# Making the low half of each weight slot in two VectorE instructions instead of one

## What is computed

```
proj = rms_norm(x) @ w_in          # block 1: 2048 x 12288, then RWKV-7 mixing and band attention
x = x + rms_norm(merged @ w_out)
proj = rms_norm(x) @ w_in_2        # block 2: sparse attention, spatial gating
x = x + merged @ w_out_2;  x = x + relu(h @ w_ff1)**2 @ w_ff2
...                                # block 3: pooling, attention, another MLP
```

## Time and profile before

| | before |
|---|---|
| median of 3 runs (lowest, highest) | 3455.51 us (3454.36, 3463.07) |
| span of the profiled execution | 3455.6 us |
| TensorE busy | 3366.9 us, 97% |
| VectorE busy | 2204.8 us, 64%, of which L2436 1368.9 us |
| ScalarE busy | 1543.8 us, 45% |
| GpSimd busy | 295.2 us, 9% |
| granted TensorE clock, mean | 0.992 |

### The profile page before, as it was taken

How to read it: one execution, slowest core, us unless ns; L and a number is a source line. 1 busy time by engine, 2 the same in 40 slices (tenths; PEclk the granted TensorE clock), 3 DMA queues, 4 the chain that set the end, 5 groups by cost and what they waited for, 6 DMA issues and landing times.

```text
span 3455.6 us, 52015 instructions
## 1 busy us (share of the span) xinstructions
PE 3366.9 (97%) x21718; PEld 2908.9 (84%) x21718; DVE 2204.8 (64%) x3040; ACT 1543.8 (45%) x2121; POOL 295.2 (9%) x318
## 2 busy tenths in 40 slices
PE   8999999999989999999999999999999999999998
PEld 7888877778878888888888888888888888888887
DVE  5567655556667576777666446655777866446654
ACT  4454433334543455544544334444454544334443
POOL 3100122220011111100100000001000100000000
PEclk9999999999989999999999999999999999999999
DMA  6554433335535545655555656555544556556554
GB/s 193 180 178 151 138 111 116 107 107 195 190 123 171 187 154 169 193 164 173 182 193 186 193 185 192 187 191 188 166 159 159 183 184 207 194 183 195 192 198 146
DMA packets 550751, 592.98 MB, mean 172 GB/s; under 512 B 16757, under 2 KB 511733, under 8 KB 550262
## 3 DMA queue, kind: packets, MB, share of 16 engines
q1 hardware_dynamic: 550518, 589.66, 52.7%
HBM read 583.24 MB, written 6.32 MB: 171 GB/s over the span
## 4 chain that ended last, share of the span: by engine, by line
PE 87%; DVE 7%; ACT 2%; issue 2%; DMA 1%; POOL 0%; SPq 0%; DVEq 0%; ACTq 0%; POOLq 0%
PE gp L2526 45%; PE gp L2530 24%; PE gp L2511 7%; PE sidep L1115 4%; PE gp L2516 3%; DVE w_parts L2436 2%; ACT w_parts L2429 1%; DVE stage L2143 0%; DMA high<-bias_rows 0%; PE sidep L570 0%; ACT lo_half L2037 0%; PE sidep L1355 0%; DVE stage L2139 0%; DMA ring<-w_branch_rwkv 0%; DVE low L2175 0%
## 5 line engine op out<-in xcount | busy, mean ns | idle before, releaser
L2436 DVE TENSOR_TENSOR w_parts<-ring,w_parts 128x1024 fp32r<-128x1024 f32 x1084 | 1368.9, 1285 | 452.8 <-ACT w_parts L2429 451.5
L2526 PE MATMUL gp<-x_parts,w_parts 128*128 128x512 f32 x5840 | 1481.7, 398 | 11.1 <-issue 5.5
L2429 ACT ACTIVATE w_parts<-ring 128x1024 fp32r<-128x1024 f32 x1084 | 1109.8, 1053 | 453.5 <-PE gp L2516 188.9
L2526 PEld LDWEIGHTS gp<-x_parts,w_parts 128*128 128x128 f32 x5840 | 1061.7, 190 | 215.6 <-issue 13.4
L2530 PEld LDWEIGHTS gp<-x_parts,w_parts 128*128 128x128 f32 x5840 | 771.8, 191 | 48.0 <-issue 6.7
L2530 PE MATMUL gp<-x_parts,w_parts 128*128 128x256 f32 x5840 | 801.4, 285 | 2.8 <-DVE w_parts L2436 2.6
L2037 ACT ACTIVATE lo_half<-gp 128x512 f32<-128x512 f32 x239 | 142.8, 598 | 892.1 <-PE gp L2526 459.4
L2526 PE MATMUL gp<-ff_parts,w_parts 128*128 128x512 f32 x1792 | 430.8, 391 | 0.0
L2526 PEld LDWEIGHTS gp<-ff_parts,w_parts 128*128 128x128 f32 x1792 | 328.6, 188 | 63.0
L2139 DVE TENSOR_TENSOR stage<-gp,lo_half 128x512 f32<-128x512 f32 x168 | 116.2, 692 | 377.3 <-ACT lo_half L2037 376.4
L2511 PE MATMUL gp<-w_parts,ff_parts 128*128 128x512 f32 x1024 | 273.7, 389 | 0.0
(11 more groups left out here) (392 smaller groups left out, 1867.1 us busy)
## 6 DMA issues: line engine op xcount, KB each, us to landing
ring<-w_in SPq DMA_DIRECT2D x220, 1024.0 KB, 5.1
ring<-w_ff SPq DMA_DIRECT2D x128, 1024.0 KB, 5.6
ring<-w_up SPq DMA_DIRECT2D x64, 1024.0 KB, 6.0
ring<-w_down SPq DMA_DIRECT2D x64, 1024.0 KB, 5.0
ring<-w_out SPq DMA_DIRECT2D x48, 1024.0 KB, 5.3
ring<-w_branch_attn SPq DMA_DIRECT2D x8, 1024.0 KB, 5.2
ring<-w_branch_rwkv SPq DMA_DIRECT2D x8, 1024.0 KB, 5.2
gate_scratch<-stage SPq DMA_DIRECT2D x16, 256.0 KB, 2.2
```

Of the source, the lines that this page charges most:

```text
L2429: act.activation(w_parts[:, q % PARTS, 0], ring[:, u % RING, SLOT * (q % 2):SLOT * (q % 2) + SLOT, :], ACT.Copy).then_inc(high_split, 1)
L2436: v.tensor_tensor(w_parts[:, q % PARTS, 1], ring[:, u % RING, SLOT * (q % 2):SLOT * (q % 2) + SLOT, :], w_parts[:, q % PARTS, 0].bitcast(F ...
L2526: return pe.matmul(gp[:, k % 2, j, :, :], w_parts[:, q % PARTS, 0, c, j * P:(j + 1) * P], operand(s, b, SLOT * n + c), start=(n == 0 and c ...
```

## The change

`split_low` gets a third argument, `part_of_slot`. It makes only half of the slot's low part, two chunks of 128x256 (so 128x512 numbers in one instruction). Part 0 waits for the high part; part 1 signals `low_split`. VectorE's main loop calls it twice for each slot, and between the calls it runs the mixer steps that are due at q + 0.17. Nothing changes for the other engines but the semaphores' timing.

```diff
-        def split_low(v, q):
+        def split_low(v, q, part_of_slot):
             if q >= n_slots:
                 return
-            u = q // 2
-            v.wait_ge(high_split, q + 1)
-            v.tensor_tensor(w_parts[:, q % PARTS, 1], ring[:, u % RING, SLOT * (q % 2):SLOT * (q % 2) + SLOT, :],
-                            w_parts[:, q % PARTS, 0].bitcast(F32), ALU.subtract).then_inc(low_split, 1)
+            u, c, w = q // 2, SLOT // 2 * part_of_slot, SLOT // 2
+            if part_of_slot == 0:
+                v.wait_ge(high_split, q + 1)
+            m = v.tensor_tensor(w_parts[:, q % PARTS, 1, c:c + w],
+                                ring[:, u % RING, SLOT * (q % 2) + c:SLOT * (q % 2) + c + w, :],
+                                w_parts[:, q % PARTS, 0, c:c + w].bitcast(F32), ALU.subtract)
+            if part_of_slot:
+                m.then_inc(low_split, 1)
...
                     side.run(q)
-                    split_low(v, q + 2)
+                    split_low(v, q + 2, 0)
+                    side.run(q + 0.17)
+                    split_low(v, q + 2, 1)
                     if ended(q) and not last_of_section(q):
                         sums_vector(v, *ended(q), 1)
                     side.run(q + 0.34)
```

More of the change, by code:

```diff
@@ L457, in start_vector @@
                 if g == 3:
-                    split_low(v, 0)
+                    for part_of_slot in range(2):
+                        split_low(v, 0, part_of_slot)
             for g in range(4, 8):
@@ L2576, in _ @@
                 side.run(-1)
-                split_low(v, 1)
+                for part_of_slot in range(2):
+                    split_low(v, 1, part_of_slot)
                 for q in range(n_slots + 1):
```

## The result

The changed kernel took 3475.96 us in the median of 4 runs (3472.40 to 3479.43), the kernel before 3457.82 us in 4 (3454.36 to 3463.07). The ratio is 1.0049, with an interval of 1.0035 to 1.0063: slower by 0.5%, where 3459 within 3450 to 3470 was forecast. The time is near that of the second rival (3472.9), and the largest single part of it is that rival's mechanism, but in six places of which none was on its list.

The account below looks back on a forecast made before the run. TensorE was taken as the bound, busy for 3366.9 of 3455.6 us. Adding 3.4 for spacing and 2.8 for GpSimd between halves, less 2.7 for moved steps, gave 3459.1, forecast as 3459 us, range 3450 to 3470.

Parts of the forecast that it names:

- the second rival: In 13 places the second half waits for a whole GpSimd instruction, 16.6 us: 3472.9 us; chance 0.19.
- 47: Low halves in VectorE's unbroken work behind TensorE's existing waits; each 0.073 us later, 3.4 us together.
- 15 slots only: Slots of 1084 whose low half ends below 0.5 us before its first low product; the median is 3 to 12.
- the 13 of the 47: Exposed low halves with GpSimd's work beside them, where a GpSimd turn between the halves could cost 0 to 16.6 us.
- 0.7 us in four places: Cost of GpSimd getting in between the halves, by L940's own 0.66 us: 2.8 us, range 0 to 16.6.
- Slots there stand ready over 8 us ahead, so that is hidden.: Behind the roots, the second half, L2143 and ScalarE's next steps come some 2.5 us later, at no cost.
- The roots' gain: At 807 us the roots (L1055) start 1.25 us earlier; TensorE's wait shrinks from 2.37 to 1.12 us.
- The spacing: Two halves take VectorE 0.073 us more per slot than one low half, 79 us in all, 3.4 on TensorE.
- The clock: 0: Shifts of half-clock stretches on TensorE counted as 0 us, with -1.7 and +3.4 for the range.
- GpSimd gets in between: A waiting GpSimd instruction runs whole between the halves in 13 places, 16.6 us: 3472.9 us; chance 0.19.
- The places pay: All four TensorE waits with a moved step vanish, 5.3 us, and the half-clock stretch at 807: 3452.0 us; chance 0.12.
- VectorE the bound: VectorE's extra 79 us come onto the path where it is full: 3534.6 us; chance 0.03.

Follow-up runs that it names:

- e10: Kernel before, with two halves and nothing between them in only six slots, the fourth of blocks 2 to 7 of down2_1: 3467.48 us, ratio 1.0025.
- e4: Kernel before, with halves directly behind one another only in the 64 slots of down2_1: 3466.10 us, ratio 1.0014.
- e7: Changed kernel, with GpSimd's adds behind blocks 1 to 6 of out2, down2_1 and out3a held until the next needed low half is made: 3467.34 us, ratio 1.0025.
- e1: Changed kernel, with halves but no place for mixer steps between them in any slot: 3482.31 us, ratio 1.0064.
- e3: Changed kernel, with halves only in the 34 slots that have steps between them, one instruction in the other 1050: 3456.98 us, ratio 1.0000.
- e5: Changed kernel, with GpSimd's adds of squares behind down2_1 replaced by a one-column write (norm not the reference's): 3469.86 us, ratio 1.0031.
- e6: Changed kernel, with GpSimd's two adds behind each block of down2_1 replaced by four memsets that read nothing: 3470.17 us, ratio 1.0036.
- e8: Changed kernel, with each slot in four instructions of 128x256 and nothing between them: 3505.00 us, ratio 1.0135.
- e2: Kernel before, whole low halves kept, with the mixer steps due at q + 0.17 run ahead of them: 3459.80 us, ratio 1.0001.
- e9: Kernel before, with two halves and nothing between them in 464 slots of nine sections where idle time had grown little or not: 3457.51 us, ratio 0.9999.

## Why the prediction was wrong

**Which low halves are exposed: the step that failed.** I counted the low halves behind waits that were already there, down to 0.06 us, and got 47. The six slots of down2_1 had no wait before that the profile shows; their low half ended 0.15 us before its products began. The 0.15 is also what lies between the end and the products where TensorE does wait for a low half (before, 826.62 to 826.76; after, 2355.83 to 2355.98), so there was no slack at all. They were among the "15 slots only" below 0.5 us, which I read as a sign of safety and did not price. The mechanism had been found, with the right moment ("a waiting GpSimd instruction gets in as soon as one VectorE instruction ends"), and it was weighed only on the 13 of the 47 with GpSimd beside them. For these six slots the price was in the trace: a GpSimd add of 1.30 us (2339.95) with nothing to hide it. Measured, it is 1.22 us, six times, 7.3 us. With that the sum would have been 3466, just past what can be told from no change. e10, e4 and e7 show it from three sides.

**The price of a place elsewhere.** I took 0.7 us in four places. The idle time at two grew by about 0.6 us, 461 and 657. At 657 us in after:
```profile
658.50 1.11 DVE L2438 TENSOR_TENSOR w_parts<-ring,w_parts 128x512 fp32r<-128x512 f32 x1 [0.80 <-ACT w_parts L2430]
659.02 1.17 POOL L952 TENSOR_TENSOR high<-high 128x256 f32<-128x256 f32 x1
659.53 1.21 DVE L2438 TENSOR_TENSOR w_parts<-ring,w_parts 128x512 fp32r<-128x512 f32 x1
661.49 0.27 PE L1116 MATMUL sidep<-high 64*64 64x64 f32 x2 [1.90 <-DVE high L1027]
```
The second half starts at 659.53 and takes 1.21 us, 0.5 of them behind L952. e1 has the same two (0.62 and 0.58), so price and mechanism were right, and the number of places was two, not four. The argument that a half is blocked no longer than a whole held for the first half alone: the second is blocked once more. At the wait behind L997, from which the 0.7 was read and where it was to show, the idle time grew by 0.06. The 0.82 us of L997 is also of another kind than the 2.19: L997 has one SBUF input, and the sentence on two inputs beside which the prediction sets it doesn't cover it.

**"Slots there stand ready over 8 us ahead, so that is hidden."** Wrong. The roots' gain of 1.27 us came as forecast (1.10 us left, 1.12 forecast), but the 2.5 us by which the rest moved back took 1.1 to 1.35 us of it again at 826. I had looked at the stock at the roots and not followed it to where it runs out. Likewise 0.46 came back at 570.9 and 0.35 at 1099. Of 2.8 us gained, about 0.6 stayed; e3, which has these and little else, ended 0.7 us of idle time below before, and the time doesn't show it.

**The spacing.** 0.073 us a slot was right. On TensorE I counted 3.4 us; the small places sum to 4.7, some of them without a wait before. Not all of these are spacing: 0.6 of them, at 1016 us, is 0 in e5 to e7, where all slots are halved too. The wait for GpSimd at 1029 us grew from 0.29 to 1.97 in after and e1, but to 0.45 in e5, e6 and e7; it follows the clock ahead of it, as shown above.

**"The clock: 0."** The stretch at half clock behind the roots went, and others came. Two stretches of after by window (length, busy by engine with counts, granted clock, DMA share, GB/s), as the earlier trace rows:
```profile
812.90:816.30 3.40, 3.00 (x25) 2.49 (x26) 2.41 (x6) 1.82 (x3) 0.00 (x0) 1.00 0.00 0
793.50:796.90 3.40, 3.40 (x43) 3.02 (x43) 2.16 (x6) 0.00 (x0) 0.00 (x0) 0.58 0.00 0
```
Over all executions the mean granted clock was 0.9906 for before (27 runs; 0.9905 and 0.9911 beside the later kernels), 0.9895 for after, 0.9876 for e1, 0.9893, 0.9886 and 0.9895 for e5 to e7, and 0.987 for e8. It was 0.9901 to 0.9911 for e2, e3, e4, e9 and e10. So it falls only in the kernels in which the slots of all sections are cut. 0.0011 of 3455 us is 3.8 us for after, from four runs that lie between 0.988 and 0.991, so its size is rough; 0.0030 is 10.4 for e1. That fits e1's 22.4 us over before against after's 18.1, with less idle time, though the intervals of the two ratios overlap. e7 adds up: 4.5 us of idle time and 3.5 of clock are 8.0, measured 8.4. That the small waits in the remaining sections do it is argued from this pattern and not shown, and which of them would, no run here tells apart.

**The rivals.** "GpSimd gets in between" is what happened, in other places and at half the size: 8.5 us (7.3 and 1.2) against its 16.6 for 13 places. That its 3472.9 is near the measured time is luck; what came back behind the moved steps, the small waits and the clock make up the remainder. "The places pay" fails by what is given back (e2: 5.1 us shrunk, 0.6 kept). "VectorE the bound" fails by its size: VectorE works for 84.9 us more and the span grew by 16.8, and e9 has 37.9 of them for nothing. A reading was also loose: of the 56.1 us of waits, 2.9 ended with the activations' low halves (L2295) and 5.9 with roots for which L419 waits, that is, with norms between the large products and not with mixer steps; the sum doesn't use it. The whole of after: 3455.6 + 14.3 idle + 2.5 clock = 3472.4, its span.

## What to carry to other kernels

When an instruction is split, price the places that have no wait yet but little slack, not only the waits that show, and look first where another engine's instruction stands ready to read the same memory. A distance that equals the signal's own time (0.15 us here) is no slack. A split gives that instruction a turn that it did not have, and the turn costs its whole length. A step moved ahead moves everything behind it back: follow the stock from there to its lowest point before calling it hidden.

## What the runs showed of the hardware

A VectorE half of 0.69 us took 0.95 and 1.77 us beside two GpSimd adds of 128x512, and 0.69 beside four GpSimd writes of the same size (e6). Where both engines had work ready, they took turns by whole instructions: add, half, add, half. With quarters (e8) the add had one turn. The granted clock can cost nearly as much as the waits: e1 lost some 10 us to it, beside 13.9 of idle time. And it can move a wait: at 1029 us one stretch at 1.00 in place of 0.50 made a wait of 1.97 us out of 0.45.
